# RWKV-7 block in one kernel: the low-rank products of decay and a on two row halves, and the heads of the last merge on opposite halves

## What is computed

```python
h = rms_norm_2(x, norm1_g[l])
p = h @ w_in[l]
...
pc = token_shift(pc, rwkv_mu[l])
r, k, v, xw, xa, xg = _split(pc, (D_C, D_C, D_C, R_W, R_A, R_G))
w_log = -jax.nn.softplus(-(rwkv_w0[l] + jnp.tanh(xw) @ rwkv_w2[l]).astype(f32)) - 0.5
decay = jnp.exp(-jnp.exp(w_log))
a = jax.nn.sigmoid(rwkv_a0[l] + xa @ rwkv_a2[l])
g_c = jax.nn.sigmoid(xg) @ rwkv_g2[l]
...
def step(state, inp):
    r_t, w_t, k_t, v_t, kk_t, a_t = inp
    sa = jnp.einsum('bhvk,bhk->bhv', state, -kk_t)
    state = (state * w_t[:, :, None, :]
             + sa[..., None] * (kk_t * a_t)[:, :, None, :]
             + v_t[..., None] * k_t[:, :, None, :])
    y_t = jnp.einsum('bhvk,bhk->bhv', state, r_t)
```

## Time and profile before

| | us |
|---|---|
| median of 3 runs | 2866.44 |
| lowest and highest | 2864.52, 2867.47 |
| the profiled execution | 2864.96 |
| its span, first to last instruction | 2863.2 |
| TensorE busy | 2818.1 |
| GpSimd busy | 1657.7 |
| VectorE busy | 1559.8 |
| ScalarE busy | 676.8 |

### The profile page before, as it was taken

The page is one execution under the profiler, slowest core; times in us unless marked ns, Lnnn a source line. Parts: engine busy times, 40 slices in busy tenths (PEclk is TensorE's granted clock), DMA queues, the critical chain, the costliest instruction groups (busy, mean ns, idle before and its releaser), DMA issues.

```text
span 2863.2 us, 44335 instructions
## 1 busy us (share of the span) xinstructions
PE 2818.1 (98%) x18030; PEld 2239.2 (78%) x18030; DVE 1559.8 (54%) x2283; ACT 676.8 (24%) x1158; POOL 1657.7 (58%) x1332
## 2 busy tenths in 40 slices
PE   8999999999999999999999999999999999999998
PEld 6767787888877767878888777877787787788886
DVE  7888875555236664453333385665465556662342
ACT  4443212000023442120000034233323333310000
POOL 4435577787865334667677745344444434676774
PEclk9999999999999999999999999999999999999999
DMA  7334543444322112232223321112112211222221
GB/s 280 104 119 133 202 164 109 146 148 151 128 91 79 41 62 71 74 103 96 96 96 103 99 74 62 57 64 69 51 60 69 71 54 68 77 96 98 100 96 59
DMA packets 89588, 280.50 MB, mean 98 GB/s; under 512 B 12318, under 2 KB 23326, under 8 KB 89246
## 3 DMA queue, kind: packets, MB, share of 16 engines
q1 hardware_dynamic: 85904, 274.70, 28.4%
q10 hardware_dynamic: 3502, 3.26, 0.6%
HBM read 275.80 MB, written 2.62 MB: 97 GB/s over the span
## 4 chain that ended last, share of the span: by engine, by line
PE 91%; DVE 6%; issue 1%; ACT 1%; DMA 0%; SPq 0%; DVEq 0%; ACTq 0%
PE ps L358 25%; PE ps L360 24%; PE ps L359 24%; PE ps L1404 3%; PE ps L1212 2%; PE ps L1222 2%; PE ps L1242 2%; PE ps L1449 1%; DVE first_mod L1718 1%; PE ps L1037 1%; PE ps L1033 1%; PE ps L1034 1%; PE ps L1526 0%; DVE mg L1813 0%; PE ps L1368 0%
## 5 line engine op out<-in xcount | busy, mean ns | idle before, releaser
L592 POOL TENSOR_TENSOR wR<-raw,wR 128x512 fp32r<-128x512 f32 (+1 forms) x866 | 1198.3, 1403 | 68.7 <-ACT wR L649 31.7
L588 POOL CAST wR<-raw 128x1024 fp32r<-128x1024 f32 (+3 forms) x462 | 465.2, 1007 | 1105.2 <-PE ps L360 983.6
L358 PE MATMUL ps<-hR,wR 128*128 128x512 f32 x2224 | 901.5, 405 | 6.9 <-DVE hR L1739 6.9
L359 PE MATMUL ps<-hR,wR 128*128 128x512 f32 x2224 | 868.5, 390 | 0.0
L360 PE MATMUL ps<-hR,wR 128*128 128x512 f32 x2224 | 868.2, 390 | 0.0
L358 PEld LDWEIGHTS ps<-hR,wR 128*128 128x128 f32 x2224 | 418.0, 188 | 112.5 <-issue 21.0
L360 PEld LDWEIGHTS ps<-hR,wR 128*128 128x128 f32 x2224 | 418.0, 188 | 89.4
L359 PEld LDWEIGHTS ps<-hR,wR 128*128 128x128 f32 x2224 | 418.5, 188 | 81.7 <-issue 4.3
L1697 DVE SCALAR_TENSOR_TENSOR xT<-ps,lm,xT 128x512 f32<-128x512 f32 x32 | 24.0, 751 | 216.0 <-PE ps L360 215.9
L358 PE MATMUL ps<-act_f,wR 128*128 128x512 f32 x352 | 137.7, 391 | 0.0
L360 PE MATMUL ps<-act_f,wR 128*128 128x512 f32 x352 | 136.9, 389 | 0.0
(11 more groups left out here) (394 smaller groups left out, 4189.0 us busy)
## 6 DMA issues: line engine op xcount, KB each, us to landing
raw<-in_weights_dram SPq DMA_DIRECT2D x468, 512.0 KB, 3.3
first_mod<-in_weights_dram SPq DMA_DIRECT2D x16, 512.0 KB, 10.3
raw<-in_weights_dram SPq DMA_DIRECT2D x50, 128.0 KB, 2.4
raw<-in_weights_dram SPq DMA_DIRECT2D x16, 256.0 KB, 2.8
raw<-in_weights_dram SPq DMA_DIRECT2D x8, 384.0 KB, 10.2
xT<-in_x_dram SPq DMA_DIRECT2D x1, 2048.0 KB, 9.3
rpb_wide<-bias_copies ACTq DMA_DIRECT2D x16, 128.0 KB, 4.3
out_dram<-xT SPq DMA_DIRECT2D x4, 512.0 KB, 2.6
```

Source lines behind the costliest of these rows:

```text
L358: mm(out, w_hi, r_hi, start=first, stop=False)
L359: mm(out, w_hi, r_lo, start=False, stop=False)
L588: nc.gpsimd.tensor_copy(wR[:, u, 0, 0:cols], raw[:, r % RING, 0:cols]).then_inc(hi_done, 1)
L592: ins = nc.gpsimd.tensor_tensor(wR[:, u, 1, part], raw[:, r % RING, part], wR[:, u, 0, part], ALU.subtract)
```

## The change

**First part.** w's and a's six matmuls are emitted together, in w's place: for each of the three passes one matmul on row half 0 for w and one on row half 1 for a. w's result goes to bank 4 (`W_BANK`, the bank that VectorE later fills with kk) and a's to bank 2 (`A_BANK`). w keeps its claim of bank 0, a makes none, and both still count one evacuation of their old bank. So g, behind w on bank 0, and r, behind a on bank 1, claim one count less (`before_last`). ScalarE waits for v's shift before it takes a, so that the counts of bank 1 come in order.

**Second part.** The off block of head 0 goes to partitions 64 to 127 and that of head 1 stays on 0 to 63. x6 of head 0 runs on row and output half 1, that of head 1 on row and output half 0, both into bank 2. t6 of head 0 reads row half 1 and that of head 1 row half 0, both write output half 0, in banks 2 and 3. VectorE writes one further 64x256 result, the second inverse of head 1 on partitions 0 to 63. The off and x6 copies become two of 64x256 each. On ScalarE the vtok copy moves ahead of Exp, and the x6 copies stand between Exp and Tanh.

```diff
--- before.py
+++ after.py
@@ -281,6 +281,7 @@
 PAIR = SC
 K_FACTOR, K_ROOT, KK, A_KK, DECAY, Y = 2, 3, 4, 5, 5, 6
+A_BANK, W_BANK = K_FACTOR, KK
@@ -845,7 +846,8 @@
-                return A(dst, ps[:, ACC + b, :], func, **kw).then_inc(bank_free[b], 1)
+                src = ps[:, {"w": W_BANK, "a": A_BANK}.get(kind, ACC + b), :]
+                return A(dst, src, func, **kw).then_inc(bank_free[b], 1)
@@ -904,6 +906,7 @@
                 take("w", m, ps[:, DECAY, :], ACT.Tanh, bias=vec(half2, W_W0), scale=0.5)
+                act.wait_ge(shifted, 5 * m + 2)
                 take("a", m, aB[:], ACT.Tanh, bias=vec(half2, W_A0), scale=0.5)
@@ -922,19 +925,23 @@
-                copy(m, "off", off[0:64].rearrange("p h a n -> p h (a n)"), ps[0:64, 5:7, 0:256])
+                act.wait_ge(mat_out, len(COPIES) * m + COPIES.index("off") + 1)
+                A(flat(off[64:P, 0]), ps[64:P, 5, 0:256], ACT.Copy)
+                A(flat(off[0:64, 1]), ps[0:64, 6, 0:256], ACT.Copy).then_inc(mat_in, 1)
...
+                copy(m, "vtok", flat(vtok), ps[:, SUM, :])
                 act.wait_ge(la_ready, m + 1)
                 A(sg2[:, 3, :], sg2[:, 1, :], ACT.Exp)
+                act.wait_ge(mat_out, len(COPIES) * m + COPIES.index("x6") + 1)
+                A(flat(off[64:P, 0]), ps[64:P, 2, 0:256], ACT.Copy)
+                A(flat(off[0:64, 1]), ps[0:64, 2, 256:512], ACT.Copy).then_inc(mat_in, 1)
                 A(sg2[:, 1, :], sg2[:, 1, :], ACT.Tanh, scale=-1.0).then_inc(lru_ex, 1)
-                copy(m, "vtok", flat(vtok), ps[:, SUM, :])
-                copy(m, "x6", off[64:P].rearrange("p h a n -> p (h a n)"), ps[64:P, 2, :])
-                copy(m, "t6", mats["TT"][0:64, :, :, 64:P], ps[0:64, 3, :].rearrange("p (h a n) -> p h a n", h=2, a=CH))
+                copy(m, "t6", mats["TT"][0:64, :, :, 64:P], ps[0:64, 2:4, 0:256].rearrange("p h (a n) -> p h a n", a=CH))
@@ -990,14 +997,14 @@
-            def claim(p):
+            def claim(p, before_last=False):
...
                 else:
-                    pe.wait_ge(bank_free[b], ((p - b).half() + C_BANK).value())
+                    pe.wait_ge(bank_free[b], ((p - b).half() + (C_BANK - (1 if before_last else 0))).value())
                 return ACC + b
@@ -1331,20 +1338,28 @@
-                    if kind in ("w", "a", "g", "wa", "wi"):
...
-                        three_passes(MM, ps[:, bank, :], w[0], w[1], src[lo_:hi_, 0, :], src[lo_:hi_, 1, :], True, True
-                                     ).then_inc(signal, 1)
+                    if kind == "w":
+                        slot_, _ = need_tile(Count(t)), claim(Count(P_MIX + p))
+                        if m == 0:
+                            pe.wait_ge(xin_ready, 2)
+                        for n, (part, moved) in enumerate(((0, 0), (0, 1), (1, 0))):
+                            for rows_, out_bank in ((half_of(0), W_BANK), (half_of(1), A_BANK)):
+                                mm = MM(ps[:, out_bank, :], wR[rows_, slot_, part, 0:P], xaR[rows_, moved, :], start=(n == 0), stop=(n == 2))
+                                if n == 2:
+                                    mm.then_inc(part_ready, 1)
+                        yield
+                    elif kind == "a":
+                        yield
+                    elif kind in ("g", "wa", "wi"):
+                        col, src = {"g": (1, xgR), "wa": (0, uR), "wi": (1, uR)}[kind]
+                        slot_, bank = need_tile(Count(t)), claim(Count(P_MIX + p), kind == "g")
...
                     else:
-                        yield from steps_of(t, P_MIX + p, range(KD), h_hi, h_lo, signal)
+                        yield from steps_of(t, P_MIX + p, range(KD), h_hi, h_lo, signal, before_last=kind == "r")
@@ -1485,7 +1500,7 @@
                                 rows_ = slice(64 * h, 64 * h + 64)
-                                mm = MM(ps[0:64, 5 + h, 64 * cc:64 * cc + 64], aB[rows_, cc * P:cc * P + 64],
+                                mm = MM(ps[half_of(1 - h), 5 + h, 64 * cc:64 * cc + 64], aB[rows_, cc * P:cc * P + 64],
@@ -1504,16 +1519,16 @@
-                        mm = MM(ps[64:P, 2, 256 * h + 64 * cc:256 * h + 64 * cc + 64], off[0:64, h, cc, :], tt[0:64, 0, h, cc, :],
-                                start=True, stop=True)
+                        mm = MM(ps[half_of(1 - h), 2, 256 * h + 64 * cc:256 * h + 64 * cc + 64], off[half_of(1 - h), h, cc, :],
+                                tt[half_of(1 - h), 0, h, cc, :], start=True, stop=True)
...
-                        mm = MM(ps[0:64, 3, 256 * h + 64 * cc:256 * h + 64 * cc + 64], off[64:P, h, cc, :], mats["TT"][64:P, h, cc, 64:P],
-                                start=True, stop=True)
+                        turned = tt[0:64, 0, 0, cc, :] if h else mats["TT"][64:P, 0, cc, 64:P]
+                        mm = MM(ps[0:64, 2 + h, 64 * cc:64 * cc + 64], off[half_of(1 - h), h, cc, :], turned, start=True, stop=True)
@@ -2278,12 +2293,13 @@
-                        v(TT(first(0, 0)[0], first(0, 64)[1], first(0, 64)[0], ALU.add))
+                        v(TT(first(0, 64)[0], first(0, 64)[1], first(0, 64)[0], ALU.add))
...
-                        TT(full[64:P, :, :, 64:P], src[64:P], tt[64:P, 1], ALU.add).then_inc(mat_used, 1)
+                        v(TT(full[64:P, :, :, 64:P], src[64:P], tt[64:P, 1], ALU.add))
+                        TT(tt[0:64, 0, 0], src[64:P, 1], tt[64:P, 1, 1], ALU.add).then_inc(mat_used, 1)
```

More of the change, by code:

```diff
@@ L1085, in sum_squares, with steps_of @@
                        ).then_inc(sq_used, 1)
-            def steps_of(t, p, ks, r_hi, r_lo, signal, col=0, width=P):
-                slot, bank = need_tile(Count(t)), claim(Count(p))
+            def steps_of(t, p, ks, r_hi, r_lo, signal, col=0, width=P, before_last=False):
+                slot, bank = need_tile(Count(t)), claim(Count(p), before_last)
                 for n, k in enumerate(ks):
@@ L1333, in mix_dense @@
                     t, signal = G_B2 + slot, tile_used if last else part_ready
-                    if kind in ("w", "a", "g", "wa", "wi"):
-                        lo_, hi_, col, src = {"w": (0, 64, 0, xaR), "a": (64, P, 0, xaR), "g": (0, P, 1, xgR),
-                                              "wa": (0, P, 0, uR), "wi": (0, P, 1, uR)}[kind]
-                        slot_, bank = need_tile(Count(t)), claim(Count(P_MIX + p))
+                    if kind == "w":
[13 more added lines that the diff above has]
+                        slot_, bank = need_tile(Count(t)), claim(Count(P_MIX + p), kind == "g")
@@ L1338, in mix_dense @@
                         if kind == "wa":
                             pe.wait_ge(u_ready, m + 1)
-                        elif kind == "w" and m == 0:
-                            pe.wait_ge(xin_ready, 2)
-                        w = [wR[lo_:hi_, slot_, part, col * P:(col + 1) * P] for part in range(2)]
-                        three_passes(MM, ps[:, bank, :], w[0], w[1], src[lo_:hi_, 0, :], src[lo_:hi_, 1, :], True, True
-                                     ).then_inc(signal, 1)
+                        three_passes(MM, ps[:, bank, :], weight(slot_, 0, col * P), weight(slot_, 1, col * P), src[:, 0, :], src[:, 1, :],
+                                     True, True).then_inc(signal, 1)
```

## The result

| | before | after |
|---|---|---|
| median, us | 2865.48 (4 runs beside the kernel after) | 2847.77 (4 runs) |
| lowest to highest | 2864.52 to 2867.47 | 2847.69 to 2847.87 |
| the profiled execution | 2864.96 | 2847.78 |
| its span | 2863.2 | 2846.0 |

The ratio is 0.9936, 95% interval 0.9924 to 0.9947. The forecast was 2850.0 us, the range 2847.0 to 2856.0.

The account below looks back on a forecast made before the run. TensorE's queue, busy 2818.1 of 2863.2 us, was taken as the bound. Steady stages' 13.65 and stage 0's 2.9 made 16.5 us, giving 2848.5 against the profiled execution or 2849.9 against the median; forecast 2850.0, range 2847.0 to 2856.0.

Parts of the forecast that it names:

- The pairs' 0.89: w's and a's six matmuls run as three slots, 0.33 and 0.23, then 0.33 to g: 0.89 us.
- Rival 1: The w and a pairs don't overlap; only the claims gain: 4.2 us less, 2854.1; chance 0.08.
- The covers: Slack left ahead of TensorE's next waits: 0.25 us at xb's claim of bank 0, 0.8 at r.
- 0.50 a group: In the last merge, x6 and t6 each fall from 1.14 to off's 0.64 us.
- The copies: In the last merge, one 64x512 copy (0.59 us) becomes two of 64x256, 0.38 each, 0.17 more in all.
- The charge of 0.05 at t6: x6's copies end at 2027.50, TensorE reaches t6 at 2027.56; 0.05 us charged for possible waiting, up to 0.2.
- Rival 2: x6 stays serial because both heads write one bank: 7 x 0.5 us less, 2853.4; chance 0.06.
- Rival 3: Thin covers at xb's claim (0.25) and x6's copies (0.06) break: 6.4 us less, 2856.3; chance 0.09.
- Rival 4: ScalarE's new wait ahead of a delays g's evacuation; lateness beyond 0.25 us stops TensorE at xb: 2875.9; chance 0.02.
- Rival 5: Nothing gained, since something other than quadrants and claims sets the groups' times: 2866 us; chance 0.05.
- The sum: Seven steady stages at 1.0 + 0.50 + 0.45 give 13.65 us, stage 0 2.9, together 16.5.

Follow-up runs that it names:

- pairs_old_claims: The changed kernel with the full claims for g and r again, w and a still pairs: median 2854.7 us, ratio 0.9963 to the kernel before.
- x6_two_banks: The changed kernel with head 1's x6 written to bank 3 and read there by ScalarE: median 2847.9 us, ratio 0.9938 to the kernel before.
- old_act_order: The changed kernel with ScalarE's old order Exp, Tanh, vtok, x6's copies: median 2856.8 us, ratio 0.9968 to the kernel before.
- late_g: The changed kernel with two more 128x512 copies on ScalarE ahead of a's Tanh: median 2853.6 us, ratio 0.9958 to the kernel before.
- p1_only: The kernel before with only the first part of the change, last merge as before: median 2857.0 us, ratio 0.9969 to the kernel before.
- p2_only: The kernel before with only the second part of the change, w and a as before: median 2859.3 us, ratio 0.9976 to the kernel before.
- before_st0: The kernel before plus x6 and vtok copies ahead of ScalarE's decay wait, and stage 0's decay preparation moved off v's shift: median 2862.1 us, ratio 0.9986.

## Why the prediction held, and where its steps were off

**Part 1.** w's first to r's first matmul was to be 1.65 us and is 1.69; with r's first step 1.92 instead of 2.97, a gain of 1.05 where 1.08 was worked out and 1.0 taken. The pairs' 0.89 was exact. g's three take 0.80, not 0.77, since g's first step is 0.34, the step after a change of row mode, and not r's 0.31. The mechanism, claims that open when an evacuation ends, was in the starts of the earlier trace rows: three starts 0.14 to 0.15 us behind an evacuation's end. pairs_old_claims shows it: with the six matmuls in 0.89, g's claim alone holds back 0.88 us a stage. Over the whole stage part 1 gives 1.07 to 1.09 (97.90 to 96.83, and 98.80 to 97.71).

**Rival 1** fell, with the pairs in 0.89. The nearest rows, two score matmuls on row halves, carried over to the other number form.

**The covers.** xb was to have 0.25 and has 0.37. The difference is ScalarE: the prediction let g's evacuation end 0.16 earlier, because a is ready with w, and it ends 0.26 earlier in the stage (6.63 us behind its start, not 6.89). a's Tanh now follows w's by 0.59, where it was 0.84. r waited nowhere in a steady stage, as said. In stage 0 it waits for v's shift; that gained 1.78 to r's second matmul instead of 1.88, because the first step after a wait stays at 0.31.

**Part 2.** 0.50 a group was too much: x6 and t6 fell from 1.07 to 0.61 by starts, or 1.14 to 0.68 by durations, where off's 0.64 had been taken as the measure. Two groups gave 0.92, of which 0.04 is lost again in two small steps later in the stage. The 0.04 between x6 and off is not the bank (x6_two_banks). The starts of single records show where it sits: in both groups every further record of a head follows 0.058 us behind the last, but in x6 and t6 the second follows 0.107 behind the first (2017.359 and 2017.466). Off stands right behind other 64x64 records, x6 and t6 behind a full matmul, so this is again the first step after a change of row mode, and the prediction took its measure from a group that doesn't pay it. Off itself went from 0.57 to 0.56: nothing, as said. **The copies** of 0.38 were as estimated. The charge of 0.05 at t6 didn't arise; the step ahead of it is 0.33 in both kernels, which is the change of row mode. The cover, 0.06 in the prediction, is 0.08 by old_act_order, which runs into it.

**Rival 2** fell with x6 at 0.61 in one bank, and x6_two_banks, with the second bank, changed nothing. **Rival 3**: neither cover broke; late_g and old_act_order show what it would have cost. **Rival 4** was tested for its slope, and is right in that; the delay itself did not come. **Rival 5** fell, with both parts at work.

**The sum.** Steady stages were to gain 1.95 each and gained 1.97. That this is so close is luck, two errors that cancel: some 0.07 too little for part 1 and some 0.05 too much for part 2. Stage 0 was to give 2.9 and gave 2.77. Against the profiled execution that made 2848.5, and 2847.8 came; the rest is the longer stage 3 and the later begin of stage 0 in the profile before, neither of them foreseen. The forecast of 2850.0 leaned on the median, 1.5 above the profiled execution, as if those 1.5 would stay. They went, and this is most of the 2.2 us between forecast and median. The runs of the kernel before fall into two levels, 2864.5 to 2864.8 and 2865.8 to 2866.8, with a few above, and the kernel after has one. A fall of the clock in stage 0 (1.55 to 1.64 us) makes such a step, and an earlier fall at the end makes one of 0.9. Where the kernel before has its fall was not seen, since its profiled execution is of the lower level. Nor is the shorter wait for v's shift enough to take it away: p1_only has the same 0.64 at r as the kernel after, and five of its seven runs are 1.5 to 2.4 above the lowest, with the fall behind t6 in its profile. Why the kernel after has one level, in four runs, stays open.

## What to carry to other kernels

Where TensorE is full, look at starts and not at idle time: a start 0.15 us behind an evacuation's end is a wait, though nothing is printed, and a result in another bank, so that the next claim is older, can be worth much more than the overlap by itself (0.88 against 0.19 a stage here), though the overlap is what lets the next product start so early. Three matmuls on one row half followed by three on the other needed no interleaving, eight and eight did; and a wait between the two groups holds the second back. When a group gets shorter, the copy that feeds the next one is due earlier by the same amount, so its place in ScalarE's queue has to be moved with it; and a one-off wait of 1.5 us or more can cost as much again, since the clock fell behind some of them.

## What the runs showed of the hardware that was not expected

- TensorE starts a matmul whose row half is free beside one that stands three or four places before it, and no farther in these runs: w and a take 0.89 us issued in turn and 0.90 apart, eight records of each head 0.61 in turn and 0.89 apart. By the Trainium skill (TensorE: Matmul & The Clock Gate, Part 3, the list "What overlaps and what doesn't") matmuls start strictly in program order; these runs show otherwise for matmuls on different row halves.
- A fall of the granted clock between matmuls, 0.63 to 0.72 in a row of 4 us, cost 1.55 to 1.64 us in the four profiles that have one between 60 us and the last matmuls (p1_only, p2_only, old_act_order, before_st0). In the first three it came within 2 us of a wait of 1.5 to 2.7 us; waits of 1.5 us at four other places never had one.
- A change between full matmuls and half-row ones shows in two steps, the one into the new kind and the one behind it: 0.32 and 0.107 us into x6 (2017.04, 2017.36, 2017.47), where 0.23 and 0.058 are usual, and 0.33 and 0.34 from w and a into g.
- The same release costs unlike times in two places: a product starts 0.14 to 0.15 us behind the end of the 128x512 evacuation that frees its bank, t6 0.05 behind the end of its 64x256 copy (old_act_order).
